# One opening stage in place of four, the first norm applied inside the projection, and memory attention in the fox pipeline

## The chip, the core and the metric

The kernel runs on one core of one Trainium2 chip. The metric is device time in microseconds (us) of one execution; lower is better. Engines are named PE or TensorE (matmuls), DVE (VectorE), ACT (ScalarE), POOL (GpSimd) and SP (SyncE, which issues the plain transfers). The 16 DMA engines move data between device memory and the cores' SBUF.

## What is computed

Two transformer blocks over 512 tokens of width 1024, batch 1, all in f32. Cut to what matters here:

```python
mod = silu(c) @ w_ada + b_ada                      # 1024 -> 6144: shifts, scales and gates
sh1, sc1, gt1, sh2, sc2, gt2 = split(mod, 6)
h = rms_norm(x, norm_mix) * (1 + sc1) + sh1        # first norm, modulated
proj = h @ w_in                                    # feeds latent attention, an RWKV scan, gates
x = x + gt1 * mixer(proj)
x = x + gt2 * experts(rms_norm(x, norm_ffn) * (1 + sc2) + sh2)     # top 16 experts for each of 8 heads
# second block: a mixer of three attentions, and experts again
o_fox = softmax(q k^T + forget + causal) v         # 8 heads of 64
o_swa = windowed attention with alibi and sinks    # 8 heads of 64
o_mem = softmax(q_mem k_mem^T) v_mem               # 4 heads of 128, over 256 memory rows
x = x + gated_sum(o_fox, o_swa, o_mem) @ w_out
x = x + experts(rms_norm(x, g))
```

## The kernel before

Activations lie transposed: xT, hT and z have the feature in the partition (128 of them) and 512 tokens along the free axis, one chunk for every 128 features; x has 8 chunks. The program is a row of stages. Each is a block in which every engine has its own instruction list; engines meet at the end of a block, and within one they meet at semaphores only.

**Opening.** load_stage (L108) issues six transfers on SP's queue, the last of them x (2 MB), and waits for all of them. ada_stage (L121) computes the first four of the twelve groups of mod: SP loads a 2 MB tile of w_ada for each group in three buffers (L140), DVE multiplies its 8 chunks with silu(c) and adds them up in a chain (L165, L167), and PE sums the result over the partitions with eight small matmuls (L151). At its end DVE adds the bias (L173). gain_stage (L2210, L2211) makes (1 + scale) x gain. norm_stage n1 (L408) squares the 8 chunks of x on ACT (L429), sums them over partitions on PE with a matrix of ones (L440), and DVE takes the mean (L450), ACT the root (L432), DVE the reciprocal (L452), and then for each chunk DVE scales (L454) and, chained to it, adds the shift (L457).

**First projection.** project_stage p1 (L461) multiplies hT with 34 column tiles of w_in. Each operand is split in a rounded high part and a low rest, and three matmuls make one product. Ahead of its loop ACT copies each chunk of hT to its high part (L513) and DVE subtracts to get the low one (L574); ACT and DVE then split the first weight tile (L510, L550), and PE begins (L531). PE waits for all eight low parts.

**Gather slots.** From the first expert layer to the end the expert work is hosted by all other stages. One slot is one of the 128 (head, choice) columns of 128 tokens: POOL issues an indirect transfer of 128 rows of 8 KB into one of eight pair buffers (L232), DVE makes the dot product with the down row (L298), ACT the activation and a diagonal matrix (L271, L278), and PE adds the weighted up row (L252), four slots behind DVE. A buffer is asked for again when PE has finished with it. shared_out gives each stage a share of a fixed number of slots by its length in MIXER_LENGTHS, and Beats spreads a stage's share over its steps; on each engine a slot's instructions stand in the list behind those of the host's step.

**Second mixer.** It runs twice, for half of the tokens each (h0 and h1). Its stages in order: norm, projection p2, head norms, transposes, attention of fox and windowed heads (foxa, 32 items), attention over the memory (mema, 8 items), gate projection pg (24 chunks), merge, output projection, norm, and the choice of experts. attention_stage (L815) is a software pipeline with four steps more than items. At step n PE makes the scores of item n (L868), transposes the weights of item n-2 (L878) and multiplies those of n-3 with the values (L887); DVE finds the maximum of n (L943, L946), normalizes n-1 (L953, L954) and copies the result of n-4 (L960); ACT makes the exponentials (L910) and copies the transposed weights (L923). Hosted, it has two score banks and one result bank. The results of neighbouring fox items lie in different partitions of that bank; those of memory items fill all 128, so each waits for the copy of the one before.

mema loads the memory's keys and values (1 MB) and the first tile of pg at its start (L848, L195), and PE, ACT and DVE each wait for that load before their first instruction. In h1, foxa also loads kept keys and values of h0.

## Time and profile before

| what | us |
|---|---|
| median of three runs | 4124.55 |
| the runs | 4119.18 to 4124.9 |
| the profiled execution | 4123.17 |
| its span in the trace | 4121.0 |
| granted TensorE clock, mean | 0.821 |
| busy: PE, DVE, POOL, ACT | 3087.5, 2398.7, 1167.9, 910.3 |

All rows come from the profiled execution. Its span leaves out 2.2 us that its own time has; its time is 1.4 us under the median. Busy shares are of the whole span and average over stages with different limits.

### The profile page before, as it was taken

The page shows a single profiled execution, that of the slowest core. Times are in us where ns is not written, and L with a number is a line of the kernel's source. Part 1 is how long each engine was busy: PE and PEld are TensorE (multiplying, and loading weights), DVE is VectorE, ACT ScalarE, POOL GpSimd, SP SyncE. Part 2 cuts the span into 40 slices and gives each one's busy share as a digit, 9 for nine tenths or more (in the row PEclk, how much of TensorE's full clock was granted, in tenths as well). Part 3 has the DMA queues.
Part 4 walks back from the last instruction along what each step waited for, and adds up shares of the span by engine and source line. Part 5 has one row for each costly group of instructions (what it writes and reads, how often), then busy time and mean ns, then how long its engine had stood idle before and what let it go on. Part 6 is the DMA issues. An engine that isn't in the chain of part 4 may idle for free. (4 is left out here: it accounts for less than half of the span.)

```text
span 4121.0 us, 49937 instructions
## 1 busy us (share of the span) xinstructions
PE 3087.5 (75%) x18158; PEld 1500.1 (36%) x18158; DVE 2398.7 (58%) x6100; ACT 910.3 (22%) x2477; POOL 1167.9 (28%) x1029
## 2 busy tenths in 40 slices
PE   3985597794676666889698875989699886676666
PEld 2863393441131111543365531633265541111111
DVE  5557744328746777457545479456645468755554
ACT  1113331101211111126412111125512111111111
POOL 0000000003443444323233243222333234444443
PEclk8998798896787776987899986978899997666666
DMA  4530001227999999988799897986799999999998
GB/s 166 183 106 1 5 4 49 68 67 306 405 416 367 416 416 414 380 336 324 295 416 367 331 394 308 362 327 233 273 395 387 355 379 404 419 420 416 420 419 355
DMA packets 201682, 1247.03 MB, mean 303 GB/s; under 512 B 25108, under 2 KB 28820, under 8 KB 66980
## 3 DMA queue, kind: packets, MB, share of 16 engines
q0 software_dynamic: 147456, 1073.81, 65.2%
q1 hardware_dynamic: 53992, 170.17, 11.2%
q8 instruction: 138, 2.26, 0.2%
q14 instruction: 96, 0.79, 0.1%
HBM read 1239.39 MB, written 4.46 MB: 302 GB/s over the span
## 5 line engine op out<-in xcount | busy, mean ns | idle before, releaser
L252 PE MATMUL held_acc<-held_pair,held_diag 64*64 64x512 f32 x8192 | 1412.2, 787 | 602.1 <-ACT held_diag L278 563.9
L232 POOL DMA_INDIRECT held_pair<-in_experts,held_expert x1024 | 1164.1, 1137 | 2412.1 <-PE held_acc L252 1859.5
L298 DVE CUSTOM_DVE_ANT_0 held_pair<-held_pair,held_hrow 128x1024 f32<-128x1024 f32 x1024 | 1248.5, 1223 | 771.9 <-DMA held_pair<-in_experts,held_expert 750.8
L252 PEld LDWEIGHTS held_acc<-held_pair,held_diag 64*64 64x64 f32 x8192 | 271.3, 158 | 1469.7 <-ACT held_diag L278 1251.3
L278 ACT ACTIVATE held_diag<-held_bands,held_weight 128x64 f32<-128x64 f32 x1024 | 347.8, 340 | 1425.7 <-DVE held_weight L293 1409.3
L271 ACT ACTIVATE held_bent<-held_dot 128x2 f32<-128x2 f32 x512 | 104.0, 203 | 747.6 <-DVE held_dot L298 726.3
L1727 PE MATMUL c_ps<-held_hT,c_w 128*128 128x256 f32 (+1 forms) x480 | 149.6, 467 | 0.0
L1209 POOL TENSOR_TENSOR rsolve_decays<-rsolve_ident,rwkv_dend 128x2048 f32<-128x2048 f32 x1 | 3.6, 3613 | 512.0 <-DMA rsolve_ident<-in_id 512.0
L617 PE MATMUL pgh_ps<-held_hT,pgh_w 128*128 128x256 f32 x608 | 141.2, 385 | 2.2 <-DMA pgh_w<-in_w_in 2.2
L617 PE MATMUL p2h_ps<-held_hT,p2h_w 128*128 128x256 f32 x576 | 133.9, 386 | 0.0
L617 PEld LDWEIGHTS pgh_ps<-held_hT,pgh_w 128*128 128x128 f32 x608 | 112.4, 190 | 45.3 <-issue 27.6
L1771 DVE COPY held_room<-c_ps 128x256 f32<-128x256 f32 (+1 forms) x48 | 24.6, 513 | 176.0 <-PE c_ps L1727 176.0
L531 PE MATMUL p_ps<-p_hhi,p_whi 128*128 128x512 f32 x272 | 107.9, 397 | 21.6 <-DVE p_wlo L550 21.6
L617 PEld LDWEIGHTS p2h_ps<-held_hT,p2h_w 128*128 128x128 f32 x576 | 106.5, 190 | 42.2 <-issue 29.2
L1727 PE MATMUL c_ps<-held_hT,held_first_tile 128*128 128x256 f32 (+1 forms) x288 | 97.1, 496 | 27.7 <-PEq L416 27.7
L1727 PEld LDWEIGHTS c_ps<-held_hT,c_w 128*128 128x128 f32 x480 | 92.5, 198 | 60.9 <-issue 52.3
L533 PE MATMUL p_ps<-p_hhi,p_wlo 128*128 128x512 f32 x272 | 106.8, 393 | 0.0
L532 PE MATMUL p_ps<-p_hlo,p_whi 128*128 128x512 f32 x272 | 106.8, 393 | 0.0
L293 DVE TENSOR_TENSOR held_weight<-held_bent,held_gate 128x2 f32<-128x2 f32 x512 | 79.8, 156 | 17.9 <-ACT held_bent L271 11.6
L271 ACT ACT_TABLE_LOAD x67 | 86.0, 1283 | 1.2
L1727 PEld LDWEIGHTS c_ps<-held_hT,held_first_tile 128*128 128x128 f32 x288 | 60.0, 214 | 67.6 <-issue 60.8
L298 DVE DVE_READ_ACCUMULATOR2_ANT held_dot<- 128x1 f32 x1024 | 84.0, 82 | 0.0
(472 smaller groups left out, 3680.8 us busy)
## 6 DMA issues: line engine op xcount, KB each, us to landing
pgh_w<-in_w_in SPq DMA_DIRECT2D x38, 512.0 KB
p2h_w<-in_w_in SPq DMA_DIRECT2D x36, 512.0 KB
p_raw<-in_w_in SPq DMA_DIRECT2D x34, 512.0 KB, 3.6
p_w_ada<-in_w_ada SPq DMA_DIRECT2D x16, 1024.0 KB, 7.0
held_pair<-in_experts,held_expert POOLq DMA_INDIRECT x1024
held_first_tile<-in_w_in SPq DMA_DIRECT2D x20, 512.0 KB
c_w<-in_w_peer_q SPq DMA_DIRECT2D x20, 512.0 KB
...
```

What stands on the lines that cost most here:

```text
L232: pool.indirect_dma_start(self.pair[m % BUFS][:], None, self.layers[t // TT][0], bass.IndirectOffsetOnAxis(ap=self.expert[:, t % TT, s:s + ...
L252: last = pe.matmul(self.sum_of(i)[to * BAND:(to + 1) * BAND], diag[band, :], up[band, turn * WIDE:(turn + 1) * WIDE], start=s == 0, stop=s ...
L271: act.activation(self.bent[:, t % 2, at], self.dot[:, t % 2, at], self.layers[t // TT][1]).then_inc(self.bent_made, 1)
L278: act.activation(self.diag[m % DIAGS][:], self.k.bands[:], ACT.Copy, scale=self.weight[:, t % 2, s:s + 1]).then_inc(self.diag_made, 1)
L293: dve.tensor_tensor(self.weight[:, t % 2, at], self.bent[:, t % 2, at], self.gate[:, t % TT, at], ALU.mult).then_inc(self.weighed, 1)
L298: ins = dve.tensor_tensor_reduce(down, down, self.hrow[:, t % TT, :], 1.0, 0.0, ALU.mult, ALU.add, self.dot[:, t % 2, s:s + 1])
L531: pe.matmul(out, hi, hhi[:, c, :], start=c == 0, stop=False)
L532: pe.matmul(out, hi, hlo[:, c, :], start=False, stop=False)
L533: last = pe.matmul(out, lo, hhi[:, c, :], start=False, stop=c == kc - 1)
L617: last = pe.matmul(ps[n % 4][:, 0:tokens], w[n % WEIGHT_TILES][:, c, :], act_in[:, c, :], start=c == 0, stop=c == kc - 1)
L1727: last = pe.matmul(ps[n % 2][:, 0:tokens], w[n % W][:, c, :], hT[:, c, :], start=c == 0, stop=c == DC - 1)
L1771: dve.tensor_copy(qT[:, n, :], ps[n % 2][:, 0:tokens]).then_inc(used, 1)
```

## The change

The first loads, the first groups of mod, the gain and the sum of squares of the first norm become one stage. SP issues the columns, the first w_ada tile, x, the other three w_ada tiles (four buffers now, with no waits between them) and then the small tables. ACT squares x as it lands, PE sums it ahead of its product matmuls, and DVE places the mean behind its second group and the reciprocal behind its third. The application of the norm moves into p1: DVE scales a chunk, ACT adds the shift while it rounds to the high part, and DVE adds the shift again while it subtracts. Two scalings run ahead.

In the second mixer the eight memory items are appended to the 32 of foxa. Their keys and values go to chunks of z that are free by then and are loaded behind the other loads of that stage; PE waits for them at the first memory item. The first tile of pg is fetched in foxa as well. The stage's length is 52 where there were 48 and 4, so it hosts the slots of both.

The diff, cut to its core ("..." marks what is left out):

```diff
+def opening_stage(nc, k, columns, norm_gain, loads, xT, x_in, ccol, w_ada, bcol, mod, groups, sc, gain, rstd):
+        sq = [r.sb(f"sq{u}", [P, S]) for u in range(2)]
+        w = [r.sb(f"w{u}", [P, DC, 512]) for u in range(groups)]
-                for dst, src in pairs:
-                    sp.dma_start(dst, src).then_inc(loaded, 16)
-                sp.wait_ge(loaded, 16 * len(pairs))
-def ada_stage(nc, k, ccol, w_ada, bcol, mod, groups, sc):
...
-            @block.sync
-            def _(sp):
+                sp.dma_start(columns[0], columns[1]).then_inc(columns_in, 16)
                 for n in range(groups):
-                    if n >= 3:
-                        sp.wait_ge(summed, n - 2)
-                    sp.dma_start(w[n % 3][:], w_ada[n]).then_inc(w_ready[n % 3], 16)
+                    sp.dma_start(w[n][:], w_ada[n]).then_inc(w_ready[n], 16)
+                    if n == 0:
+                        sp.dma_start(xT[:], x_in).then_inc(x_landed, 16)
+                for dst, src in loads:
+                    sp.dma_start(dst, src).then_inc(others_in, 16)
+                sp.wait_ge(others_in, 16 * len(loads))
             @block.scalar
             def _(act):
+                act.wait_ge(columns_in, 16)
                 act.activation(sig[:], ccol, ACT.Sigmoid).then_inc(sig_ready, 1)
+                act.wait_ge(x_landed, 16)
+                for c in range(DC):
+                    if c >= 2:
+                        act.wait_ge(sq_summed, c - 1)
+                    act.activation(sq[c % 2][:], xT[:, c, :], ACT.Square).then_inc(sq_ready, 1)
+                act.wait_ge(mean_ready, 1)
+                act.activation(mean[:], mean[:], ACT.Sqrt).then_inc(root_ready, 1)
             @block.tensor
             def _(pe):
+                pe.wait_ge(ones_made, 1)
+                for c in range(DC):
+                    pe.wait_ge(sq_ready, c + 1)
+                    pe.matmul(ss[:], k.ones[:], sq[c % 2][:], start=c == 0, stop=c == DC - 1).then_inc(sq_summed, 1)
...
                 for n in range(groups):
-                    dve.wait_ge(w_ready[n % 3], 16 * (n // 3) + 16)
+                    dve.wait_ge(w_ready[n], 16)
...
                     ins.then_inc(summed, 1)
+                    if n == 1:
+                        dve.wait_ge(sq_summed, DC)
+                        dve.tensor_scalar(mean[:], ss[:], 1.0 / D, EPS, ALU.mult, ALU.add).then_inc(mean_ready, 1)
+                    if n == 2:
+                        dve.wait_ge(root_ready, 1)
+                        dve.reciprocal(rstd[:], mean[:])
+                link(dve.tensor_tensor(mod[:, 0:4 * groups], ps[:, 0:4 * groups], bcol[:, 0:4 * groups], ALU.add))
+                link(dve.tensor_scalar(gain[:], mod[:, DC:2 * DC], 1.0, None, ALU.add))
+                dve.tensor_tensor(gain[:], gain[:], norm_gain, ALU.mult)
...
                 for c in range(kc):
-                    act.activation(hhi[:, c, :], act_in[:, c, :], ACT.Copy).then_inc(h_hi, 1)
+                    if normed:
+                        act.wait_ge(scaled, c + 1)
+                        act.activation(hhi[:, c, :], act_in[:, c, :], ACT.Identity, bias=normed[3][:, c:c + 1]).then_inc(h_hi, 1)
+                    else:
+                        act.activation(hhi[:, c, :], act_in[:, c, :], ACT.Copy).then_inc(h_hi, 1)
...
+                def scale(c):
+                    src, gain, rstd, _ = normed
+                    dve.scalar_tensor_tensor(act_in[:, c, :], src[:, c, :], gain[:, c:c + 1], rstd[:], ALU.mult, ALU.mult).then_inc(scaled, 1)
+
+                if normed:
+                    scale(0)
+                    scale(1)
                 for c in range(kc):
+                    if normed and c + 2 < kc:
+                        scale(c + 2)
                     dve.wait_ge(h_hi, c + 1)
-                    dve.tensor_tensor(hlo[:, c, :], act_in[:, c, :], hhi[:, c, :].bitcast(F32), ALU.subtract).then_inc(h_lo, 1)
+                    if normed:
+                        ins = dve.scalar_tensor_tensor(hlo[:, c, :], act_in[:, c, :], normed[3][:, c:c + 1], hhi[:, c, :].bitcast(F32), ALU.add, ALU.subtract)
+                    else:
+                        ins = dve.tensor_tensor(hlo[:, c, :], act_in[:, c, :], hhi[:, c, :].bitcast(F32), ALU.subtract)
+                    ins.then_inc(h_lo, 1)
...
+    sunk_to = N if sunk_to is None else sunk_to
+    sunken = lambda n: sunk_from <= n < sunk_to
     hosting = beats is not None
     SC, PO = (2, 1) if hosting else (3, 2)
-    apart = PO == 2 or all(items[n][4] % per != items[n + 1][4] % per for n in range(N - 1))
+
+    def lands(n):
+
+        if n >= sunk_to:
+            return 0, P, whole_T, items[n][4]
+        per = P // vdim
+        return items[n][4] % per * vdim, vdim, sunk_T if n >= sunk_from else oT, items[n][4] // per
+
+    apart = lambda n: PO == 2 or n < sunk_to and lands(n)[0] != lands(n - 1)[0]
...
@@ -850,6 +888,8 @@
                     fetch(sp)
                 for dst, src in sunk_loads:
                     sp.dma_start(dst, src).then_inc(sinks_loaded, 16)
+                for dst, src in late_loads:
+                    sp.dma_start(dst, src).then_inc(late, 16)
...
+                    if n == sunk_to:
+                        pe.wait_ge(late, 16 * len(late_loads))
...
+                    if n >= 2 or n and not apart(n):
+                        pe.wait_ge(taken, n - 1 if apart(n) else n)
...
+                        if sunken(n):
...
-            spare = [room[:, Y_GATE + 2 * u:Y_GATE + 2 * u + 2, :].rearrange("p a n -> p (a n)") for u in range(4)]
+            sunk_to = len(items)
+            mkv = z[:, Y_FK:Y_SQ, :]
+            items += [(z[:, Y_MQ + head, here(t)], mkv[:, head, :], None, [mkv[:, 4 + head, j * P:(j + 1) * P] for j in range(2)], head, t - first, None)
+                      for head in range(GH) for t in tiles]
+            spare = [room[:, c:c + 2, :].rearrange("p a n -> p (a n)") for c in (Y_SKV, Y_FF, 3 * DC + 4, 3 * DC + 6)]
             attention_stage(nc, own("foxa"), k, items, FH, FD, foxT, sunk_from=sunk_from, sinks=sinks, sunk_T=swaT, beats=beats["attention"], spare=spare,
+                            sunk_to=sunk_to, whole_T=memT, late_loads=[(mkv, memory)],
+                            fetch=lambda sp: first_tile.fetch(sp, ins["w_in_2"][Y_GATE:Y_N]),
                             sunk_loads=[(alibi[:], ins["alibi"]), (sinks[:], ins["swa_sinks"].to_broadcast([P, SH]))],
                             loads=kept if half else [], saves=[] if half else [(there, here_) for here_, there in kept])
-        with ExitStack() as mem:
-            mkv = Room(nc, mem, own("mem")).sb("mkv", [P, 8, NMEM])
-            items = [(z[:, Y_MQ + head, here(t)], mkv[:, head, :], None, [mkv[:, 4 + head, j * P:(j + 1) * P] for j in range(2)], head, t - first, None)
-                     for head in range(GH) for t in tiles]
-            attention_stage(nc, own("mema"), k, items, GH, GD, memT, loads=[(mkv[:], memory)], beats=beats["mema"],
-                            spare=[room[:, c, :] for c in [Y_GATE] + list(range(3 * DC + 4, 4 * DC))],
-                            fetch=lambda sp: first_tile.fetch(sp, ins["w_in_2"][Y_GATE:Y_N]))
...
-MIXER_LENGTHS = {"n3": 2, "p2": 40, "hn": 15, "vt": 0, "attention": 48, "mema": 4, "pg": 42, "mg": 21, "po": 12, "n4": 2,
+MIXER_LENGTHS = {"n3": 2, "p2": 40, "hn": 15, "vt": 0, "attention": 52, "pg": 42, "mg": 21, "po": 12, "n4": 2,
...
-        load_stage(nc, "first", [(k.ident[:], ins["ident"]), (k.columns[:], ins["columns"]), (k.causal[:], ins["causal"]), (k.pair_ones[:], ins["pair_ones"]), (k.bands[:], ins["bands"]),
-                                 (xT[:], ins["xT"].rearrange("(c p) t -> p c t", p=P))])
         sc = r.sb("silu", [P, DC])
-        ada_stage(nc, k, cols("c"), ins["w_ada"], cols("b_ada"), mod, EARLY_ADA, sc)
-        gain_stage(nc, "g1", gain, cols("norm_mix"), mod[:, DC:2 * DC])
-        norm_stage(nc, "n1", k, xT, DC, D, gain, hT, shift=mod[:, 0:DC])
         with ExitStack() as mixer:
             m = Room(nc, mixer, "mix")
             z = m.sb("z", [P, Z_N, S])
+            rstd = z[:, Z_ROPE, :]
+            opening_stage(nc, k, (k.columns[:], ins["columns"]), cols("norm_mix"), loads, xT, ins["xT"].rearrange("(c p) t -> p c t", p=P),
+                          cols("c"), ins["w_ada"], cols("b_ada"), mod, EARLY_ADA, sc, gain, rstd)
             project_stage(nc, "p1", k, ins["w_in"], hT, DC, Z_N, z,
-                          ada=(ins["w_ada"], cols("b_ada"), mod, EARLY_ADA, sc))
+                          ada=(ins["w_ada"], cols("b_ada"), mod, EARLY_ADA, sc), normed=(xT, gain, rstd, mod[:, 0:DC]))
```

lands(n) gives the partitions and the target of item n: as before for the first 32, all 128 and memT for the memory items. Where the cut lines test n >= sunk_from they test sunken(n) now.

## Rows read from the trace of the kernel before

**Rows 1.** The page's slices: granted TensorE clock and DMA share, 40 equal parts.
```profile
PEclk8998798896787776987899986978899997666666
DMA  4530001227999999988799897986799999999998
```

**Rows 2.** Timeline of the opening: start, length (us), engine, line, tiles, count, idle before.
```profile
3.09 0.43 SPq L117 DMA_DIRECT2D held_xT<-in_xT  x1
...
13.44 14.57 SPq L140 DMA_DIRECT2D ada_w<-in_w_ada  x4
...
21.66 0.49 DVE L165 TENSOR_SCALAR ada_acc<-ada_w,held_silu 128x512 f32<-128x512 f32 x1 [6.52 <-DMA ada_w<-in_w_ada]
...
22.18 5.48 DVE L167 SCALAR_TENSOR_TENSOR ada_acc<-ada_w,held_silu,ada_acc 128x512 f32<-128x512 f32 x7
...
27.57 0.48 DVE L165 TENSOR_SCALAR ada_acc<-ada_w,held_silu 128x512 f32<-128x512 f32 x1
...
47.34 0.17 DVE L173 TENSOR_TENSOR held_mod<-ada_ps,held_columns 128x16 f32<-128x16 f32 x1 [1.96 <-PE ada_ps L151]
...
49.28 10.17 PE L440 MATMUL n_ss<-n_sq,held_ones 128*128 128x512 f32 x16 [1.98 <-ACT n_sq L429]
...
60.88 3.35 DVE L452 RECIPROCAL n_rstd<-n_root 128x512 f32<-128x512 f32 x1 [0.70 <-ACT n_root L432]
...
64.27 0.75 DVE L454 SCALAR_TENSOR_TENSOR held_hT<-held_xT,held_gain,n_rstd 128x512 f32<-128x512 f32 x1
...
73.34 0.49 DVE L457 TENSOR_SCALAR held_hT<-held_hT,held_mod 128x512 f32<-128x512 f32 x1
...
74.18 4.27 ACT L513 ACTIVATE p_hhi<-held_hT 128x512 fp32r<-128x512 f32 x8 [13.33 <-PEq L416]
...
74.84 4.91 DVE L574 TENSOR_TENSOR p_hlo<-held_hT,p_hhi 128x512 fp32r<-128x512 f32 x8 [1.02 <-ACT p_hhi L513]
...
81.02 0.79 PE L531 MATMUL p_ps<-p_hhi,p_whi 128*128 128x512 f32 x1 [21.57 <-DVE p_wlo L550]
```

**Rows 3.** Windows: length, busy us by engine, clock, DMA, GB/s; three stages h0, two h1.
```profile
1859.50:2006.60 147.10, 124.24 (x608) 46.31 (x608) 108.65 (x340) 97.05 (x223) 59.74 (x46) 0.79 0.90 334
2006.60:2043.60 37.00, 18.51 (x96) 10.43 (x96) 14.85 (x50) 13.32 (x34) 3.37 (x4) 0.75 0.48 182
2043.60:2172.60 129.00, 126.06 (x704) 81.50 (x708) 61.87 (x140) 16.77 (x62) 43.25 (x39) 1.00 1.00 408
2954.20:2994.00 39.80, 21.88 (x96) 12.82 (x96) 14.84 (x50) 13.43 (x34) 3.36 (x4) 0.67 0.50 194
2994.00:3120.70 126.70, 125.81 (x704) 81.42 (x708) 60.10 (x128) 16.77 (x62) 43.96 (x39) 1.00 1.01 412
```

**Rows 4.** Timeline of memory attention in h0.
```profile
2016.70 2.07 PE L868 MATMUL memah_ps<-memh_mkv,held_room 128*128 128x256 f32 x4 [16.27 <-DMA memh_mkv<-memory_scratch]
...
2029.11 0.42 DVE L943 TENSOR_REDUCE memah_nmax<-memah_ps 128x1 f32<-128x256 f32 x1 [1.30 <-PE memah_ps L868]
...
2030.37 1.22 DVE L298 CUSTOM_DVE_ANT_0 held_pair<-held_pair,held_hrow 128x1024 f32<-128x1024 f32 x1
...
2032.90 0.42 DVE L943 TENSOR_REDUCE memah_nmax<-memah_ps 128x1 f32<-128x256 f32 x1 [1.30 <-PE memah_ps L868]
...
2035.47 0.42 DVE L943 TENSOR_REDUCE memah_nmax<-memah_ps 128x1 f32<-128x256 f32 x1 [1.30 <-PE memah_ps L868]
```

**Rows 5.** Windows of the opening, while the first tile of w_ada lands.
```profile
14.00:16.00 2.00, 0.00 (x0) 0.00 (x0) 0.17 (x1) 0.93 (x2) 0.00 (x0) 1.00 0.80 221
16.00:21.66 5.66, 0.00 (x0) 0.00 (x0) 0.00 (x1) 0.00 (x0) 0.00 (x0) 1.00 0.99 420
```

**Rows 6.** Unchained 128x512 operations of DVE (L1088): shortest, median, longest ns; first and last.
```profile
L1088 DVE SCALAR_TENSOR_TENSOR mix_z<-rprep_d,held_columns,mix_z x14: 742/743/750, 442.7 to 451.4; 128x512 f32<-128x512 f32 x14
```

**Rows 7.** The page's DMA issues: the projection's weight tiles, median us to landing.
```profile
p_raw<-in_w_in SPq DMA_DIRECT2D x34, 512.0 KB, 3.6
```

**Rows 8.** Waits in attention h0, 1860 to 2007: us in total, times, longest.
```profile
DVE held_pair L298 <- DMA held_pair<-in_experts,held_expert: 6.0, 4, 3.7
```

54 lines of the change are left out of this document (23 added, 31 removed).

## The prediction, made before any run of the changed kernel

> **What bounds the kernel now.** I began with the page's slices [rows 1]. The 16 DMA engines are nearly idle over the first fifth of the span and nearly full from there to the end: the expert gathers set the pace once they run, and what lies ahead of them is a serial chain of stages. The granted TensorE clock never reads as steadily low, so it is not the first suspect. Two stretches interest the change: the opening, and the two places in the second mixer where memory attention stands as a stage of its own.
>
> In the opening the timeline [rows 2] is to be read as a chain. w_ada is only asked for at 13.44, when the first loads are in. DVE starts on it at 21.66 and does four groups without a gap (21.66 to 27.57 is 5.91 us for one: 0.49 and 5.48). The norm then begins: squares and TensorE's sum take 10.17 us, the reciprocal 3.35, and eight pairs of an application and a shift follow, 64.27 to 73.83. Only then does the projection's stage begin, at 74.18, and its first matmul starts at 81.02. TensorE does nothing else of use before that, so that start is what the opening is worth; all later stages wait for it in turn.
>
> In the mixer the windows [rows 3] show three neighbours in each half. Fox attention takes 147.1 us for 46 gather slots (the L252 and L298 work of one expert column for 128 tokens), memory attention 37.0 and 39.8 us for 4 slots each, and the gate projection some 129 and 127 us. In the memory stage the DMA engines are half idle (0.48 and 0.50); in the gate projection they are full (1.00 and 1.01, 408 and 412 GB/s) and TensorE as well (126.06 of 129.0). The steps [rows 4] say why the memory stage is slow: its first matmul waits 16.27 us for keys that are asked for as the stage begins, and as every engine's first act waits on them, the hosted gather slots stand still too, with nothing for POOL to refill.
>
> **Opening, part by part.** What is removed: three stages with their changes, the wait of all w_ada transfers for all first loads, and the eight shifts. What is added: eight scalings and a shift folded in the split, sixteen DVE operations where eight were.
>
> When data lands. The first w_ada tile (2.10 MB) was usable 8.2 us after its issue [rows 2]. In that time 0.44 MB moved in the first two microseconds and 2.38 MB at 420 GB/s [rows 5], so a transfer is complete when 0.72 MB of what follows it has moved too. SP's issues stand some 0.46 us apart (x, the sixth, was issued at 3.09 [rows 2]), so in the new order the columns go at 0.8 and w0 at 1.2, then x, w1, w2, w3. With half a microsecond for the columns, w0 is usable at 9.9. x ends behind 4.2 + 0.72 MB: 0.6 to the first byte, 2.0 for 0.44 MB, 10.7 for the rest, so 15.0. w1 ends behind 6.3 + 0.72 MB: 5.0 us later, 20.0. w2 and w3 land at 25 and 30, ahead of need.
>
> DVE's chain. w0 runs 9.9 to 15.8. Then DVE waits for w1 until 20.0: the stall at 21.66 has moved here and is 4.2 us long. w1 to 25.9. TensorE's sum of squares starts 0.7 us after x and takes the same 10.17: 15.0 to 25.9, beside w1, and costs nothing as long as x lands in time; without w1's cover it would be 10 us. The mean takes 0.69, to 26.7. The first product is queued on TensorE behind the sum and takes 1.9 us (the idle time in front of L173 [rows 2]), and DVE's third group waits for it: 27.9 to 33.8. The reciprocal comes between third and fourth group, on the path: 3.35, to 37.2. w3 to 43.1, product 1.96, mod and two gains of 0.17 with their waits 0.6, stage change 0.4: the projection's stage begins at 46.1. The square root and its table load lie beside the third group. The small loads that now come last are behind w3 by 30 and wait for nothing.
>
> Projection's head. Before, from stage start to first matmul 6.84 us [rows 2]. Now DVE issues sixteen 128x512 operations; unchained ones of this kind start 0.67 us apart (14 from 442.7 to 451.4 [rows 6]): 10.7. ACT's eight conversions (4.27) keep two chunks ahead and are hidden, as is the first weight tile (a median of 3.6 us to landing [rows 7]). The weight split (1.22) and its wait end it: 12.1. First matmul at 58.2 against 81.02: **22.8 us gained**.
>
> Here a page can be weighed. The row gives 8.2 us for 2.10 MB. The Trainium skill, "DMA: Bandwidth & Descriptors", anatomy of one DMA, fits 2.0 us plus bytes over 436 GB/s, which makes 6.8. By it w1 would land at about 17.7 and the opening would gain some 2.3 us more; the row speaks against it.
>
> **Mixer, part by part.** Total gather slots stay: the shares are 48 + 4 before and 52 now, so the other stages keep theirs. What goes is a start with its load (16.27 us of TensorE waiting in the first half) and four steps of filling and draining. What comes are eight steps and four slots more in the fox pipeline, and 1.57 MB (keys and values 1.05, a weight tile 0.52) moved forward on SP's queue.
>
> The price of a step: reductions at 2032.90 and 2035.47 stand 2.57 apart with no slot between; 2029.11 to 2032.90, with one slot (2030.37), is 3.79, so a slot costs 1.22 [rows 4]. As a test: 36 steps and 46 slots at these prices give 148.6 us, the row has 147.1 [rows 3]. Eight steps and four slots: 20.6 + 4.9 = 25.5 us. The halves gain 37.0 - 25.5 = 11.5 and 39.8 - 25.5 = 14.3, together **25.8 us**.
>
> The wait that TensorE now makes ahead of step 33 is for a transfer issued 32 steps earlier and costs nothing; behind it would stand all its gather work. The 1.57 MB go ahead of or behind the alibi table while DVE waits for landings hardly at all there (6.0 us in 147 [rows 8]); they are taken at nothing, covered by the four slots in flight. Uncovered they are 1.57 MB / 334 GB/s = 4.7 us a half.
>
> What is given back: in its stalled stage the DMA engines moved 182 x 37.0 = 6.73 MB and 194 x 39.8 = 7.72 MB [rows 3], where four slots and the loads need 4.19 + 1.57 = 5.76. The surplus, 0.97 and 1.96 MB, was a head start into the gate projection. At 410 GB/s it is 2.4 and 4.8 us. That stage shows full DMA engines and a full TensorE; between nothing and 7.2 us I take all 7.2, since the DMA share is at its ceiling. Mixer net: **18.6 us**.
>
> **Sum.** 22.8 + 18.6 = 41.4 us off the profiled execution's 4123.2, so 4081.8; the median shown is 1.4 us above it, so 4083. A measurement of this kernel can tell about 0.2% (8 us) from no change.
>
> **Rivals.**
> (a) Nothing is given back, as TensorE and not DMA bounds the gate projection. For: 126.06 of 129.0 us busy. Against: 1.00 DMA share. 25.8 + 22.8 gained: 4076. Chance 0.2.
> (b) Attention has no room for the moved transfers. For it: the DMA share there is already 0.90. Against: at 334 GB/s, where the next stage draws 408 [rows 3]. Twice 4.7 us less gain: 4092. Chance 0.15. In a sentence aside, the Trainium skill's main page (Key Constraints) says that DMAs of all issuing engines run on the same 16 engines and interleave, which would be this rival's mechanism.
> (c) The opening's transfers share the engines instead of following each other, and w1 lands with w3 at about 28 to 30. For: no row shows several landings. Against: the first tile was usable at 21.66 though two more had been issued. DVE would then end at about 30 + 3 x 5.91 + 3.35 = 51.1 instead of 43.1: 4091. Chance 0.1.
> (d) Slower: TensorE's clock. The attention stage had a granted clock of 0.79, memory attention 0.75 and 0.67 [rows 3]. If the pauses of the memory steps (its value products wait for DVE's copy each step) drew the whole merged stage down, its 124.24 us of TensorE work would grow as 0.79 over the new clock. The gain is gone and 8 us more are lost when both stages give up 25 us each, which is at 0.66; at 0.5 they would give up 72 each (4227). Against: slots go on between the steps, and eight steps cannot slow the 36 ahead of them. Chance 0.02.
> (e) The change doesn't do what it says: a wait or a late landing keeps DVE or SP at the old times, and less than 8 us is gained. Chance 0.03.
> The forecast itself has 0.5.
>
> **How the numbers follow.** The opening is worth 15 (c) to 25, the mixer 9 (b) to 26. Most of what these allow lies between 4070 and 4099; beyond it are (d), (e) and the meeting of (b) and (c). Faster by over 0.2% is everything but (d) and (e): 0.95; same 0.03; slower 0.02.
>
> **What would show it.** First projection matmul near 58 us, a DVE wait of about 4 us for w_ada near 16, the sum of squares ending near 26, a first matmul 12 us behind its stage's start. In the mixer one attention stage of about 173 us in the first half in place of 184, no TensorE wait for memory keys, and a gate projection of 129 to 132 us. The prediction is wrong if x or w1 lands 5 us late, if gate projection grows by more than the 2.4 and 4.8 us of its head start, or if DVE begins to wait for landings in attention.

## The result, and where the time went

The changed kernel takes 4062.3 us, the median of four runs (4055.29 to 4067.72), against 4121.86 for the kernel before on the same chip. The ratio is 0.9855, with a 95% interval of 0.9834 to 0.9876: 60 us less, between 51 and 68. Forecast were 41 us, and the range ended at 4070. The direction was right; the mixer's term of the sum was too small.

The profiled execution took 4057.91 us, with a span of 4056.1 and a mean granted clock of 0.825. The page's slices, to be held against [rows 1]:

```profile
PEclk8998698896787777987899986988999987766666
DMA  5510002118999999988899997987999999999998
```

A slice is 101 us, more than the whole gain, so the slices hardly tell the two kernels apart; the stages have to be read one by one.

**The opening.** Its timeline, the same columns as [rows 2]:

```profile
9.54 0.49 DVE L168 TENSOR_SCALAR ada_acc<-ada_w,held_silu 128x512 f32<-128x512 f32 x1 [6.36 <-DMA ada_w<-in_w_ada]
...
16.46 10.04 PE L150 MATMUL ada_ss<-ada_sq,held_ones 128*128 128x512 f32 x16 [16.46 <-ACT ada_sq L141]
...
20.60 0.49 DVE L168 TENSOR_SCALAR ada_acc<-ada_w,held_silu 128x512 f32<-128x512 f32 x1 [5.06 <-DMA ada_w<-in_w_ada]
...
27.39 0.49 DVE L168 TENSOR_SCALAR ada_acc<-ada_w,held_silu 128x512 f32<-128x512 f32 x1 [0.17 <-PE ada_ps L154]
...
45.59 2.08 DVE L589 SCALAR_TENSOR_TENSOR held_hT<-held_xT,held_gain,mix_z 128x512 f32<-128x512 f32 x3 [0.58 <-PEq L121]
...
57.55 0.79 PE L546 MATMUL p_ps<-p_hhi,p_whi 128*128 128x512 f32 x1 [13.16 <-DVE p_wlo L565]
```

Read down the starts: first tile used at 9.54, a wait of 5.06 us for the second, the sum of squares beside it, projection stage at 45.59, first matmul at 57.55 where it was 81.02 [rows 2]. That is 23.5 us gained.

**The second mixer.** Windows from the first score matmul to the first of the gate projection, and the gate projection itself, first half and second (columns as in [rows 3]):

```profile
1837.80:2005.20 167.40, 141.29 (x705) 56.74 (x705) 122.72 (x389) 110.27 (x258) 61.64 (x50) 0.81 0.86 325
2005.20:2136.00 130.80, 128.06 (x696) 83.36 (x696) 60.62 (x138) 16.70 (x62) 42.49 (x38) 0.97 1.00 407
2740.00:2922.70 182.70, 158.29 (x825) 64.68 (x825) 131.67 (x389) 118.36 (x258) 60.44 (x50) 0.90 0.78 283
2922.70:3051.80 129.10, 126.74 (x696) 82.42 (x696) 58.98 (x126) 16.73 (x62) 43.79 (x38) 0.98 1.01 414
```

One attention of 167.4 us stands where the two stages took 183.5 (the 147.1 + 37.0 of [rows 3] less the 0.6 us ahead of the first score matmul), and one of 182.7 where the stages from 2780.1 to 2994.1 took 214.0. So attention gave 16.1 and 31.3 us where 11.5 and 14.3 were forecast. Measured to the first matmul of the merge behind it, the gate projection grew from 138.5 to 140.6 and from 135.6 to 139.0: 2.1 and 3.4 us given back (2.4 and 4.8 forecast). Together 23.5 + 47.4 - 5.5 = 65.4, and the span is 64.9 shorter. What has to be explained is the 21.6 us that attention gave beyond its forecast.

The memory steps, by DVE's reductions and hosted dot products (L309 is before's L298), first half:

```profile
1964.98 0.42 DVE L985 TENSOR_REDUCE foxah_nmax<-foxah_ps 128x1 f32<-128x256 f32 x1
1966.38 1.21 DVE L309 CUSTOM_DVE_ANT_0 held_pair<-held_pair,held_hrow 128x1024 f32<-128x1024 f32 x1
1967.52 0.41 DVE L985 TENSOR_REDUCE foxah_nmax<-foxah_ps 128x1 f32<-128x256 f32 x1
1969.01 1.22 DVE L309 CUSTOM_DVE_ANT_0 held_pair<-held_pair,held_hrow 128x1024 f32<-128x1024 f32 x1
1970.27 0.42 DVE L985 TENSOR_REDUCE foxah_nmax<-foxah_ps 128x1 f32<-128x256 f32 x1
1971.45 1.21 DVE L309 CUSTOM_DVE_ANT_0 held_pair<-held_pair,held_hrow 128x1024 f32<-128x1024 f32 x1
1972.76 0.42 DVE L985 TENSOR_REDUCE foxah_nmax<-foxah_ps 128x1 f32<-128x256 f32 x1
```

Steps 32 to 34 take 2.54, 2.75 and 2.49 us with a slot in each; the forecast had 3.79, and these three steps alone give 3.6 us a half beyond it. Later ones, in which the value products wait for DVE's copy, take 3.91, 5.05 (two slots), 3.79 and 3.79. The 1.22 us of [rows 4] hold in the later ones: step 36 takes 2.57 without a slot (in the packed kernel below), 3.79 with one and 5.05 with two. No run has steps 32 to 34 of the merged stage without a slot, so it is not shown whether the slot is free there or the step itself is shorter. A second slot is not free there: step 32 takes 5.05 us with two (packed, second half) where it takes 2.54 with one.

From here on a step is the time from one such reduction to the next. Before, 46 slots in 36 steps put two slots in eight of the steps 0 to 30; now 50 in 44 put two in four of them, 7, 14, 21 and 29 (and in step 36). The sums in us, counted from the first reduction:

| kernel | steps 0-30, h0 | h1 | 31 to gate projection, h0 | h1 |
|---|---|---|---|---|
| before | 126.1 | 153.4 | 55.6 | 56.9 |
| changed | 122.2 | 136.2 | 43.4 | 42.8 |
| slots moved to the memory stage | 121.4 | 134.8 | 54.1 | 51.1 |
| keys loaded ahead | 138.4 | 150.9 | 44.3 | 44.3 |
| packed as before (last series) | 131.8 | 149.2 | 42.0 | 37.6 |
| one less | 130.0 | 146.1 | 44.3 | 42.5 |
| two more | 117.5 | 133.5 | 42.6 | 43.7 |

About half of the surplus, 11.3 of 21.6 us, lies in steps 0 to 30, whose work the change hardly touches; 7.2 of the other 10.3 are steps 32 to 34. The third and fourth rows are kernels of the experiments below, with the border and the two stages of before. The third, with as many slots in steps 0 to 30 as the changed kernel, is within 1.5 us of it there. The fourth, with the keys loaded ahead, is within 1.6 us of it behind them (with four slots fewer there). So of the two gains, the one in steps 0 to 30 goes with the slots and the one behind them with the keys.

### The profile page after: what moved, and what is told of

It is laid out like the page before. It is cut to its first block and busy times, and to the rows that moved or that the text cites. A ratio compares the mean times of both kernels' runs of the same rounds, so it can differ in the third digit from the quotient of the medians.

```text
span 4056.1 us, 49859 instructions
## 1 busy us (share of the span) xinstructions
PE 3071.0 (76%) x18158; PEld 1490.0 (37%) x18158; DVE 2393.2 (59%) x6092; ACT 911.5 (22%) x2477; POOL 1164.3 (29%) x1029
## 5 line engine op out<-in xcount | busy, mean ns | idle before, releaser
L309 DVE CUSTOM_DVE_ANT_0 held_pair<-held_pair,held_hrow 128x1024 f32<-128x1024 f32 x1024 | 1248.4, 1223 | 790.8 <-DMA held_pair<-in_experts,held_expert 782.6
L304 DVE TENSOR_TENSOR held_weight<-held_bent,held_gate 128x2 f32<-128x2 f32 x512 | 79.7, 156 | 15.2 <-ACT held_bent L282 8.6
L282 ACT ACT_TABLE_LOAD x67 | 86.0, 1283 | 1.2
L309 DVE DVE_READ_ACCUMULATOR2_ANT held_dot<- 128x1 f32 x1024 | 83.5, 82 | 0.0
```

The lines of the kernel that those rows point to most:

```text
L282: act.activation(self.bent[:, t % 2, at], self.dot[:, t % 2, at], self.layers[t // TT][1]).then_inc(self.bent_made, 1)
L304: dve.tensor_tensor(self.weight[:, t % 2, at], self.bent[:, t % 2, at], self.gate[:, t % TT, at], ALU.mult).then_inc(self.weighed, 1)
L309: ins = dve.tensor_tensor_reduce(down, down, self.hrow[:, t % TT, :], 1.0, 0.0, ALU.mult, ALU.add, self.dot[:, t % 2, s:s + 1])
```

## The experiments

Ratios are to the kernel before, measured beside each; the changed kernel's is 0.9855 (0.9834 to 0.9876).

### The two parts alone

The first is the kernel before with the new opening and the scaled projection only; the second has the old opening and the merged attention only.

```diff
 first kernel, against the one before
-        ada_stage(nc, k, cols("c"), ins["w_ada"], cols("b_ada"), mod, EARLY_ADA, sc)
-        norm_stage(nc, "n1", k, xT, DC, D, gain, hT, shift=mod[:, 0:DC])
+            opening_stage(nc, k, ...)
+            project_stage(nc, "p1", ..., normed=(xT, gain, rstd, mod[:, 0:DC]))
 second kernel, against the one before
-"attention": 48, "mema": 4
+"attention": 52
+            items += [... for head in range(GH) for t in tiles]
+                            sunk_to=sunk_to, whole_T=memT, late_loads=[(mkv, memory)],
```

> The opening alone: one opening stage and the norm applied in the projection; the second mixer as before. By the trace of the changed kernel the first projection matmul comes 23.5 us earlier (57.55 against 81.02) and the first expert stage 24.2 us earlier. If the opening's gain is simply carried on (theory O), this kernel is 24 us faster than before. If part of what the change gained in the second mixer came from the shift in time itself (theory S), it gains more than 30.

> The merged attention alone, the opening as before. Theory O: about 40 us faster than before, nearly all of it in the two attention stages (16 us in the first half, 31 in the second) less some 2 to 3 us each in the gate projections, and nothing in other stages. Theory S: less than 30.

Measured: 0.9932 (0.9914 to 0.995), 28 us, for the opening; 0.9886 (0.9863 to 0.9908), 47 us, for the mixer. The first lies between its two theories and decides neither; the second is over the 40 of theory O, and theory S is out. Their sum, 75 us, is over the 60 of both together, though the intervals touch. The traces show one source of such scatter: with the opening alone, attention and memory, whose code is before's, took 192.3 and 207.1 us in place of 183.5 and 214.0. With the mixer's change alone the merged attention took 167.2 and 179.9 us, within 3 us of the changed kernel's. The division is clear all the same: the mixer carries more than the 18.6 us that it was given.

### Slots moved from attention to the memory stage

The kernel before, with nothing merged:

```diff
-"attention": 48, "mema": 4
+"attention": 43, "mema": 9
```

> The kernel before with only its shares changed: attention 43 and memory attention 9 in place of 48 and 4, so that attention hosts 41 slots in its 36 steps in place of 46 and memory attention 8 to 9 in 12 steps in place of 4. Theory L (the prediction's: a slot costs 1.22 us wherever it stands): attention falls by 6 us and memory attention rises by 6 in each half; no change overall within 4 us. Theory D (the second slot in one step is what costs, 3 to 4 us, and a single one 1.2 or less): attention falls by 10 in the first half and 15 or more in the second, memory attention rises by 6; the kernel is 13 to 20 us faster.

Ratio 0.9946 (0.9922 to 0.997), 22 us. The two halves from the first score matmul to the gate projection:

```profile
1862.50:2039.20 176.70, 143.05 (x705) 57.63 (x705) 122.61 (x389) 107.73 (x255) 63.24 (x49) 0.78 0.82 306
2779.00:2968.60 189.60, 161.83 (x825) 65.87 (x825) 131.59 (x389) 115.90 (x256) 60.91 (x49) 0.86 0.75 271
```

Against before's 183.5 and 214.0, this takes 6.8 and 24.4 us off by moving slots, with the stage border, the load and its wait all left in place. Steps 0 to 30 hold 35 slots for 39 and give 4.7 and 18.6 us; the rest, with four slots more, does not grow as both theories had it but shrinks by 1.5 and 5.8 (the table). A slot does not cost the same wherever it stands, which the forecast had assumed.

### The wait for the memory's keys

In the changed kernel, the keys moved among the loads that all engines wait for; in the kernel before, the keys loaded in the attention ahead while the memory stage stays apart:

```diff
 changed kernel
-late_loads=[(mkv, memory)], ... loads=kept if half else [], ...
+late_loads=[], ... loads=(kept if half else []) + [(mkv, memory)], ...
 kernel before
-sunk_loads=[(alibi...), (sinks...)]
+sunk_loads=[(alibi...), (sinks...), (mkv, memory)]
-attention_stage(nc, own("mema"), ..., loads=[(mkv[:], memory)], ...)
+attention_stage(nc, own("mema"), ...)
```

> The changed kernel with the memory's keys and values among the loads that all engines wait for at the start of the merged stage, as memory attention did before. If the removed wait is worth what the row of before shows (10 us or more a half, in which no slot moves), this kernel is 8 to 10 us slower than the changed one in the first half; in the second, where the stage waits for the kept keys anyway, 2 to 3 us for 1 MB more: 10 to 13 us in all. If the slots in flight make good for it (a refilled buffer is used later), under 5 us.

> The kernel before with memory attention still a stage of its own, but its keys and values loaded during fox attention. Theory W (the prediction's: the wait is lost time): the 16 us of TensorE's wait go, the memory stage takes 22 to 25 us in place of 37 to 40, and some of it is given back in the gate projection: 15 to 25 us faster in all. Theory B (the refilled buffers are worth nearly as much as the wait costs, as the changed kernel with the wait put back was hardly slower): the memory stage is shorter by 10 us but DVE then waits for landings in it and in the gate projection, and the kernel is only 2 to 10 us faster.

The first gave 0.9846 (0.9827 to 0.9864): not slower than the changed kernel, so the second of its two expectations held. The attention started 6 us later behind the transposes in the first half, and from the end of the transposes to the gate projection it took only 2.7 us more (171.4 for 168.7) and 3.2 in the second half (194.1 for 190.9). In the first half 3.6 us of it came back in steps 0 to 30, where the granted clock was at 1.00 from step 6 on and in the changed kernel from step 8 on. So this kernel does not price the wait. The second does: 0.9943 (0.9922 to 0.9963), 23.5 us. Its first memory score no longer waits for a transfer:

```profile
2016.75 2.05 PE L868 MATMUL memah_ps<-held_room 128*128 128x256 f32 x4 [6.18 <-PEq L840]
```

where [rows 4] has 16.27. Step 31 shrank from 29.99 and 28.09 us to 19.60 and 18.48, by 10.4 and 9.6, and all behind step 30 by 11.3 and 12.5 (the table). Theory W held. So the removed wait was worth about 20 us of the mixer's gain by itself. In the first half steps 0 to 30 took 138.4 us where before had 126.1, with the slots in the same steps; that hid the gain in this trace.

### One slot a step

The changed kernel with six slots fewer in attention, 44 in 44 steps, so that no step holds two. They went to the choice of experts, and in a later kernel to the head norms:

```diff
-"hn": 15, "attention": 52, "choose": 67
+"hn": 15, "attention": 46, "choose": 73    # first kernel
+"hn": 21, "attention": 46, "choose": 67    # second kernel
```

> The changed kernel with shares of 46 for attention and 73 for the last choice of experts in place of 52 and 67: attention then hosts 44 slots in 44 steps, one in each, and six slots a half move to the choice stage. Theory D (the second slot of a step costs about 3 us, a single one little): attention falls from 168 and 183 us to about 150 and 165, the choice stages rise by six slots at 1.2 to 2.5 us; the kernel is 6 to 20 us faster than the changed one (ratio to before near 0.982). Theory L (1.22 us a slot wherever it stands): attention falls by 7 us a half and the choice stage rises by as much; no difference.

> The changed kernel with six of the gather slots that the attention hosts given to the head norms instead (attention length 46, head norms 21). With six given to the choice of experts, attention fell by 21.7 and 12.5 us and the choice took 14 and 9 us more. Theory P (the second slot of a step is dear in attention, and a slot is cheap in a stage whose DMA engines are two thirds busy): attention 146 and 170 us as there, the head norm stage 5 to 15 us longer, the kernel 15 to 25 us faster than the changed one: ratio to the kernel before 0.978 to 0.981. Rival Q (a slot costs about 3 us of DMA and TensorE time wherever it goes, once everything is near its ceiling): head norms 16 us longer per half and the kernel within 5 us of the changed one, ratio about 0.985.

Ratios 0.9864 (0.9837 to 0.9891) and 0.9892 (0.9843 to 0.9941): neither is faster than the changed kernel. The first half's attention and the stretch from the norm behind it to the next head norms, for the first of the two; then the same stretch of the changed kernel:

```profile
1831.90:1977.60 145.70, 123.36 (x657) 51.67 (x657) 114.90 (x374) 102.24 (x245) 55.81 (x44) 0.88 0.88 326
2234.30:2686.70 452.40, 347.56 (x1843) 181.62 (x1843) 292.38 (x876) 85.72 (x259) 152.61 (x134) 0.85 0.91 358
```

```profile
2262.20:2700.30 438.10, 333.67 (x1794) 175.51 (x1794) 284.89 (x861) 83.36 (x250) 144.80 (x128) 0.87 0.90 356
```

Attention fell by 21.7 and 12.5 us, to 145.7 and 170.2, and the choice gave 14.3 and 8.7 back. With the head norms as hosts, attention took 142.2 and 164.5, 25.2 and 18.2 less, and the head norms, from the end of the projection to the first transpose, 13.4 and 15.3 us more, close to the 16 of rival Q. So a slot cost 2.2 to 2.6 us there and 1.5 to 2.4 in the choice: what is taken out of a dear step has its price elsewhere. The two traces leave a gain of 11 and 15 us by these sums, but both profiled executions (4047.61 and 4047.3 us) are the fastest of their kernel, whose others reach 4073.65 and 4088.04. By the medians the totals are nearer to theories L and Q than to D and P. For the forecast the useful number is the price in attention. The eight two-slot steps of before's second half add up to 54.69 us, and the same steps with one slot in this last kernel to 31.43: 23.26 / 8 = 2.9 us for a second slot (2.4 in the first half), where the forecast had 1.22. The slower clock that some of these steps of before have is part of that price: step 3 reads 0.66 there and 1.00 here.

### What makes the second slot dear

The changed kernel with Tanh for both Gelus, so that ACT need not change its table between the hosted activation and the softmax's exponential. It leaves the Gelu out of the computation.

```diff
-layers = [(ins["experts1"], ACT.Gelu_apprx_tanh, ...), (ins["experts2"], ACT.Gelu, None)]
+layers = [(ins["experts1"], ACT.Tanh, ...), (ins["experts2"], ACT.Tanh, None)]
```

> The changed kernel with Tanh in place of both Gelu functions of the experts (so it leaves the Gelu out), which lets ACT keep one table for the softmax's Exp and the experts. If the second slot of a step costs 3 us because ACT switches tables inside the step (theory T), the double steps fall from 6 to 7 us to under 5 and ACT's table loads in attention vanish. If it costs so much because a pair's dot product, activation, weight and diagonal go round between DVE and ACT within one step (theory R), the double steps fall by 1.3 to 2.6 us at most and stay 1.5 us above single ones.

It took 4053.11 us in a single run. In the changed kernel's first attention ACT loads tables 46 times:

```profile
L952 ACT ACT_TABLE_LOAD x23 | 29.5, 1283 | 5.0 <-PEq L1948 4.6
L282 ACT ACT_TABLE_LOAD x23 | 29.5, 1283 | 0.4
```

Here there are none, and steps 21 and 29 of the first half fell from 6.60 and 7.06 us to 4.56 and 4.59, step 14 from 4.94 to 4.41. In the second half step 29 fell from 7.30 to 4.99, steps 7 and 14 kept 5.56 and 5.93, and step 21 did not fall (5.27 and 5.65). At the full clock, steps with one slot agree within 0.3 us. So in three of the four two-slot steps of windowed heads the second slot lost 2.0 to 2.5 us with the table loads, and 0.9 to 1.3 of step 29 remain. Not all of this is the loads' own time: the granted clock of those three steps was 0.70, 0.71 and 0.75 with the loads and 1.00 without. At a clock of 1.00 both times, the kernel with two slots more (below) has 5.89 us in step 29 of the second half, 0.9 over the 4.99. And the clock is not set by the loads alone: steps 3 to 5 of the second half, one slot each, took 21.9 us here, mostly at 0.50, for 15.2. The Trainium skill, "ScalarE: Activation LUTs", What ACT_TABLE_LOAD costs, gives 1283 ns and another 1380 of draining for each load. The trace agrees on the first. It shows no drain: in the timeline of one less, below, a load starts at 1864.36, 0.01 us behind the end of ACT's copy, and the activation behind it at 1865.66, 0.02 us after the load.

### The order of the opening

Two kernels, both the changed one with x asked for behind the second tile of w_ada. In the first TensorE still sums the squares ahead of all products; in the second it makes two products first, and mean and reciprocal stand behind the four groups (in the first kernel the mean stands behind the third group and the reciprocal behind the fourth).

```diff
-                    if n == 0:
+                    if n == 1:
                         sp.dma_start(xT[:], x_in)...
 second kernel, TensorE
-                for c in range(DC): ...      # wait, sum of squares
                 for n in range(groups):
+                    if n == 2:
+                        for c in range(DC): ...      # wait, sum of squares
```

> The changed kernel with x loaded behind the second tile of w_ada, the mean placed behind the third group and the reciprocal behind the fourth. If the order of landing is what sets DVE's chain (theory O: tiles land 5 us apart in the order of issue), DVE's wait of 5.06 us before the second group shrinks to nothing, one of some 4 us appears before the third, the sum of squares ends near 31 in place of 26.5, and the first projection matmul comes 2 to 3 us earlier, near 55. If the transfers share the engines, nothing moves.

> The changed kernel with this order in the opening: columns, first w_ada tile, second, x, third, fourth; TensorE makes the first two product sums ahead of the sum of squares, and the mean, the root and the reciprocal stand behind all four groups. Theory (the order of landing plus the order on TensorE set the opening): the second tile lands at about 15, DVE makes its four groups with no wait over 1 us for a product or a tile except for the first, ends them at about 9.5 + 4 x 5.9 = 33 to 35, the reciprocal 3.35 and the rest bring the start of the projection stage to 42 to 43 us (45.6 in the changed kernel, 49.4 with the sum ahead of the products) and its first matmul to about 54.7 us. Rival (x is now late for the sum, which ends behind the groups): start at 45 to 46 again, with DVE waiting for the sum. Whole kernel: 3 us under the changed one by the theory, ratio to the kernel before about 0.984; the spread of runs may hide it, so the start of the projection stage decides.

The first, a miss: 0.984 (0.9818 to 0.9862), but in the trace its projection stage begins at 49.39, 3.8 us later than the changed kernel's, since DVE stood still for 11.25 us:

```profile
21.70 10.02 PE L150 MATMUL ada_ss<-ada_sq,held_ones 128*128 128x512 f32 x16 [21.70 <-ACT ada_sq L141]
31.55 1.84 PE L154 MATMUL ada_ps<-held_ones,ada_acc 128*128 128x1 f32 x16
32.61 0.48 DVE L168 TENSOR_SCALAR ada_acc<-ada_w,held_silu 128x512 f32<-128x512 f32 x1 [11.25 <-PE ada_ps L154]
```

Its third group needs an accumulator that the first product frees, and that product is queued behind a sum of squares which now starts at 21.70. The second kernel moves the product ahead:

```profile
21.41 1.87 PE L155 MATMUL ada_ps<-held_ones,ada_acc 128*128 128x1 f32 x8 [3.98 <-DVE ada_acc L171]
...
25.63 0.49 DVE L169 TENSOR_SCALAR ada_acc<-ada_w,held_silu 128x512 f32<-128x512 f32 x1 [4.28 <-DMA ada_w<-in_w_ada]
...
43.20 2.08 DVE L588 SCALAR_TENSOR_TENSOR held_hT<-held_xT,held_gain,mix_z 128x512 f32<-128x512 f32 x3 [0.58 <-PEq L121]
...
55.16 0.79 PE L545 MATMUL p_ps<-p_hhi,p_whi 128*128 128x512 f32 x1 [15.71 <-DVE p_wlo L564]
```

It starts its stage at 43.20 and its first matmul at 55.16, 2.4 us ahead of the changed kernel and close to the 54.7 expected. That DVE would wait for no tile was wrong: the wait has moved from the second tile to the third (4.28 us), as x now stands ahead of that one. The whole, 0.9841 (0.9809 to 0.9873), cannot show 2.4 us. With the six slots at the head norms as well:

> Both edits together: the other order of the opening (second tile ahead of x, products ahead of the sum of squares) and six slots moved from attention to the head norms. If the opening is worth 3 us and the slots 15 to 25, the kernel is 18 to 28 us faster than the changed one: ratio to the kernel before 0.977 to 0.981. If a slot costs the same wherever it goes, only the opening's 3 us remain: 0.984.

0.986 (0.9827 to 0.9893), not the 0.977 to 0.981 of the first theory: the miss of the head norms again.

### Density, parity and the clock

By now the surplus had two candidates: thinner spreading of the slots, or the TensorE clock, which had moved steps from kernel to kernel. The first kernel packs attention's slots as before; the others shift all of them by one or two, by lengths alone:

```diff
+class PackedBeats(Beats):      # 46 slots over 36 steps, then 4 over 8
 the others
-"p2": 40, "choose": 67
+"p2": 41, "choose": 66    # one more
+"p2": 39, "choose": 68    # one less
+"p2": 42, "choose": 65    # two more
```

> The changed kernel with one slot moved from the choice of experts to the projection p2, so that the attention's 50 slots in its 44 steps are the same in number and place but shifted by one in the count of all slots: where step 7 of the second half hosted an odd and then an even slot, it hosts an even and then an odd one. Theory R (which of the two slots shares a refill or a table switch decides): step 7 of the second half goes from 5.6 to about 8 us, as in the kernel before (8.6), and the others change by up to 2 us. Rival (parity is nothing, the step is slow for what TensorE's clock is there): all steps with two slots within 0.7 us of the changed kernel's. The kernel as a whole within 10 us of the changed one by both.

> The changed kernel, its attention hosting the same 50 slots a half, but 46 of them packed in the first 36 steps, as the kernel before had them, and 4 in the last 8. So steps 0 to 30 hold 39 slots again where the changed kernel's hold 35. Theory (the merge gained more than forecast because thinner spreading takes four two-slot steps out of steps 0 to 30, at some 3 us each): steps 0 to 30 take 133 to 137 us in the first half and 149 to 153 in the second (changed kernel 122.2 and 136.2), the later steps about 4 x 1.22 = 5 us less than in the changed kernel, and the whole is 12 to 20 us slower than the changed one: ratio to the kernel before 0.988 to 0.990. Rival (a slot costs 1.22 us wherever it stands and the short steps 0 to 30 of the changed kernel were the TensorE clock's doing): steps 0 to 30 about 127 and 141 us, the later ones 5 less, the whole equal to the changed kernel, 0.985.

> The changed kernel with one slot moved from the projection p2 to the choice of experts, so that the attention's slots are counted one lower (first slot 319 where it was 320); the look at one more gave 4087.8 us and attentions of 181.1 and 192.5 us where the changed kernel has 167.4 and 182.7. Theory R (the order of odd and even slot in a step decides): as one more, step 7 of the second half about 7.0, step 14 about 7.4, step 29 about 4.9, and the kernel within 5 us of whatever one more costs. Rival H (those two stages were long by the TensorE clock's history, not by parity): the two-slot steps of the second half as just said, but their sum within 3 us of the changed kernel's, with the total set by how many single-slot steps run at the lower clock: anywhere in 4050 to 4090, ratio 0.983 to 0.992.

> The changed kernel with two slots moved from the choice of experts to the projection p2: the attention's slots counted two higher, so odd and even stand in each step as in the changed kernel. Theory R: two-slot steps of the second half as in the changed kernel (7: 5.6, 14: 5.9, 21: 5.3, 29: 7.3, 36: 5.0) and the whole within 5 us of it, 0.984 to 0.987, and under that with one less. Rival H: the same steps, but the whole may fall anywhere in 4050 to 4090 with the number of steps at the lower clock.

**Packed**: 4074.43 us, 0.9899 (0.9866 to 0.9932), as the theory of density had it (0.988 to 0.990), though the interval still touches the changed kernel's. Steps 0 to 30 and the rest of the second half, the changed kernel and then the packed one:

```profile
2743.70:2879.90 136.20, 124.40 (x618) 49.65 (x611) 100.19 (x297) 92.38 (x196) 43.20 (x35) 0.89 0.75 269
2879.90:2922.70 42.80, 30.20 (x205) 13.74 (x203) 31.16 (x92) 25.98 (x63) 17.25 (x15) 0.97 0.87 323
```

```profile
2748.80:2898.00 149.20, 132.66 (x652) 52.73 (x644) 105.27 (x308) 98.14 (x204) 46.09 (x39) 0.87 0.77 273
2898.00:2935.60 37.60, 27.09 (x168) 13.24 (x169) 26.39 (x82) 25.69 (x59) 12.34 (x11) 0.95 0.81 288
```

Four slots more (POOL's count, 39 for 35) make steps 0 to 30 longer by 13.0 us, and by 9.6 in the first half, some 2.8 us a slot. In the first half the clock is not the reason: over these steps it reads 0.77 for the changed kernel's 0.76 (0.87 for 0.89 in the second). Their removal from the rest saves 5.2 and 1.4 us. That is the asymmetry that the forecast missed. The first half fell short of the 133 us expected by a little; the tail's saving of 5 us was met in the second half alone.

**Shifted by one or two.** One more gave 4087.77 us in a single run, one less 4069.97, 0.9873 (0.9835 to 0.991), two more 4053.15, 0.9844 (0.9812 to 0.9876). The intervals overlap, so a price of parity on the whole kernel is not established; the steps are plainer. In the second half, steps 7 and 14 take 5.56 and 5.92 us in the changed kernel and with two more, and 7.02 and 7.44 with one more and one less; step 36 takes 5.04 and 5.05, against 4.64 twice. Steps 21 and 29 do not repeat (5.27 and 7.30 in the changed kernel, 6.68 and 5.89 with two more), so parity is not all. Theory R held for steps 7, 14 and 36 only, and its step from one kernel to the next failed: one less is 18 us under one more, where within 5 were expected. Rival H is not refuted. In the code, the Gelu is made once for each pair of slots, at the even one. One more was expected to take step 7 to about 8 us; it came to 7.02. Step 7 of the first half with one less, where an even slot is followed by an odd one:

```profile
1864.08 0.27 ACT L965 ACTIVATE foxah_p<-foxah_pt 128x128 f32<-128x128 f32 x1
...
1864.36 1.28 ACT L282 ACT_TABLE_LOAD   x1
...
1865.66 0.20 ACT L282 ACTIVATE held_bent<-held_dot 128x2 f32<-128x2 f32 x1
1865.77 0.67 ACT L289 ACTIVATE held_diag<-held_bands,held_weight 128x64 f32<-128x64 f32 x2
...
1866.15 1.98 PE L263 MATMUL held_acc<-held_pair,held_diag 64*64 64x512 f32 x8 [1.92 <-ACT held_diag L289]
...
1868.07 0.79 PE L910 MATMUL foxah_ps<-partsh_fox_k,held_room 64*128 64x128 f32 x2
```

and with two more, where the odd one comes first:

```profile
1876.06 0.34 ACT L289 ACTIVATE held_diag<-held_bands,held_weight 128x64 f32<-128x64 f32 x1
1876.42 1.28 ACT L282 ACT_TABLE_LOAD   x1
...
1876.45 1.09 PE L263 MATMUL held_acc<-held_pair,held_diag 64*64 64x512 f32 x8 [1.10 <-ACT held_diag L289]
...
1877.47 0.48 PE L910 MATMUL foxah_ps<-partsh_fox_k,held_room 64*128 64x128 f32 x2
```

In the first, both diagonals stand behind the table load, and TensorE waits 1.92 us; in the second the odd slot's diagonal goes ahead of the load and TensorE waits 1.10. What follows is seen in windows of 5 us in the same step and of ten microseconds some way behind it: one less, two more, and then the packed kernel, whose step 7 has the same pause:

```profile
1863.00:1868.00 5.00, 3.08 (x18) 0.51 (x16) 3.80 (x10) 4.08 (x8) 1.97 (x2) 0.73 0.82 243
1873.00:1883.00 10.00, 10.00 (x35) 4.15 (x34) 5.26 (x17) 4.25 (x9) 1.87 (x2) 0.50 0.63 219
```

```profile
1874.10:1879.10 5.00, 3.90 (x30) 1.47 (x31) 4.36 (x13) 4.92 (x10) 2.93 (x3) 1.00 0.83 249
1880.00:1890.00 10.00, 10.00 (x60) 4.66 (x56) 8.78 (x26) 6.84 (x17) 5.06 (x4) 1.00 0.99 372
```

```profile
1862.88:1867.88 5.00, 3.08 (x18) 0.51 (x16) 3.80 (x10) 4.08 (x8) 1.97 (x2) 0.78 1.01 416
1872.88:1882.88 10.00, 8.30 (x49) 3.53 (x48) 6.86 (x21) 6.41 (x13) 4.67 (x4) 0.99 0.85 297
```

TensorE is busy for 3.08 of 5 us with one less, 3.90 with two more. After the first the granted clock reads 0.50, the 1.2 GHz level, and a pair of score matmuls takes 0.79 us for 0.48; steps 8 to 13, with one slot each, take 31.0 us. After the second it stays at 1.00 and they take 17.6. With one more, step 7 takes 6.98 us and the same six steps 31.0. But the packed kernel shows that the pause does not settle what comes after it: with the same 1.92 us of waiting, the same 3.08 of 5 us and the same 6.98 us for the step, its clock falls too, and is back at 1.00 after step 8 (3.98 us, then 3.22). So a fall of the clock behind this pause is seen three times; why it lasted over 31 us in two kernels and some 6 in the third is not shown, and none of it was induced by itself.

## Why the prediction was right in part and wrong in its size

**The opening** was right term by term: first tile 9.54 (forecast 9.9), second 20.60 (20.0), sum of squares from 16.46 (15.0), third group 27.39 (27.9), stage 45.59 (46.1), first matmul 57.55 (58.2); 23.5 us for 22.8. The page weighed there, "DMA: Bandwidth & Descriptors" of the Trainium skill, would have had the second tile at 17.7; the trace has 20.60, so the row of before was the better guide. The page gives that fit for transfers issued on the GpSimd path; these are SP's, so this is no test of the page's own case. Rival (c) is out: the tiles came in the order asked for, in both orders tried (with the second tile ahead of x, DVE began on it at 15.36 without a wait, and on the third at 25.63).

**The slot's price** is the step that failed: "a slot costs 1.22" [rows 4], used for every place. It was measured in the memory stage, by one step with a slot against one without, and holds there in the steps that wait for DVE's copy. The second slot of a fox or windowed step cost 2.4 to 2.9 us on average; in step 29, a windowed one, 2.3 to 2.5 of its 3.4 to 3.6 went with the exchange of ACT's table and the slower clock that came with it. The forecast also took all eight memory steps at 2.57 us and a slot on top, where steps 32 to 34 took 2.5 to 2.8 with their slot. The test beside it (36 x 2.57 + 46 x 1.22 = 148.6 against 147.1) fitted by luck: a step with one slot was priced at 3.79 us, while steps 0 to 30 with one slot each average 3.3 in the first half (102.8 us with the head norms as hosts), and a second slot at half of what it cost. In the second half the same test would have failed before any run: the same 148.6 us stand against 174.1 in the kernel before (2780.1 to 2954.2). A sum that fits does not confirm its parts.

With this the surplus falls in place. By 1.22 a slot, steps 0 to 30 should have given 4.9 us a half for the four slots that leave them, and the rest 6.6 and 9.4. Measured, by the table: 3.9 and 17.2 in steps 0 to 30, 12.2 and 14.1 behind them. In the second half the two-slot steps alone explain 15.2 of the 17.2: a second slot cost 23.26 us in all before, and (5.56 - 3.97) + (5.92 - 4.62) + (5.27 - 3.71) + (7.30 - 3.70) = 8.05 now. That is fewer second slots and cheaper ones: four in place of eight, at 2.0 us in place of 2.9. In the first half they give 9.3 by the same count, and steps 4 to 6 at a clock of 0.50 (16.1 us where before, at 1.00, had 8.9) took most of it back.

**The wait for the keys** was seen rightly; 10.4 and 9.6 us in step 31 are what its removal alone gives.

**What was given back** had the right size, 5.5 for 7.2; the reason given was at most half of it. The start of the gate projection, first half, in the changed kernel and then before:

```profile
2005.15 5.30 PE L645 MATMUL pgh_ps<-held_hT,held_first_tile 128*128 128x256 f32 x16 [5.70 <-PEq L878]
...
2014.21 5.41 PE L645 MATMUL pgh_ps<-held_hT,pgh_w 128*128 128x256 f32 x16 [2.74 <-DMA pgh_w<-in_w_in]
```

```profile
2043.65 3.69 PE L617 MATMUL pgh_ps<-held_hT,held_first_tile 128*128 128x256 f32 x16 [0.91 <-PEq L840]
...
2049.70 3.72 PE L617 MATMUL pgh_ps<-held_hT,pgh_w 128*128 128x256 f32 x16 [1.34 <-DMA pgh_w<-in_w_in]
```

The first tile's 16 matmuls take 1.6 us longer: TensorE comes out of a drain, and the granted clock reads 0.68 in the first 5 us for 1.00 before. Then TensorE waits 2.74 us for the second weight tile to land, for 1.34. In the second half it is 5.62 us for 3.69, and 2.36 for 0.83. The wait is a late landing, as a lost head start of the DMA engines would make it; the slower clock was in no term. That a stalled stage ahead is what gives the head start is not shown, and two kernels speak against it. With the keys loaded ahead the memory stage is shorter, yet the waits are 0.77 and 0.81 us and the gate projections, to the merge, 135.2 and 135.8. With slots moved to the memory stage it keeps its stall, and hosts more; the waits are 5.08 and 4.48 us, the projections 141.4 and 140.2 (before: 138.5 and 135.6).

**The moved transfers** cost nothing that the trace shows: DVE waits for no landing in steps 0 to 38 of either half, and rival (b) is out. Rival (d), a slower clock in the merged stage, did not come: it has 0.81 and 0.90, over the 0.79 and 0.84 of before's fox attention. Over steps 0 to 30 alone the clock went from 0.79 to 0.76 in the first half and from 0.84 to 0.89 in the second; with one slot in each step and the head norms as hosts it was 0.90 in the first. How much of the gain in the second half is the clock's own is not shown.

**What stays open**: why the two parts alone sum to 75 us and both together give 60, what sets steps 21 and 29, and what makes the clock come back late in one kernel and soon in another. And since steps 0 to 30 moved by up to 12 us in the first half between kernels with the same slots in them (126.1, 135.6 with the opening alone, 138.4 with the keys ahead), the split of the 21.6 us is good to about that. No kernel clearly beats the changed one; the best medians, 4053.98 with the products first and 4053.15 with two slots more, have ratios (0.9841, 0.9844) inside its interval.
